# Retention's scores and values from rounded halves in three passes, q and k kept in the hidden tile, the gate's projection issued behind each head's values

## The reference

```python
def project(a, rope):
    q, k, v, g = jnp.split(a @ w_in, [hk, 2 * hk, 2 * hk + hv], axis=-1)
    ...
    if rope is not None:
        q, k = apply_rope(q, *rope), apply_rope(k, *rope)
    k = k * RET_DK ** -0.5
    ...
def readout(o, g):
    y = rms_norm_2(o).transpose(0, 2, 1, 3).reshape(B, n, hv).astype(g.dtype)
    return (jax.nn.silu(g) * y) @ w_out
```

## Time and profile before

| | |
|---|---|
| median of 3 runs | 3059.17 us (3057.82 to 3060.34) |
| the profiled execution | 3062.67 us, of which the span is 3060.9 us |
| TensorE busy | 2918.7 us, 95% of the span |
| VectorE, ScalarE, GpSimd busy | 1477.6, 1044.0, 535.0 us |
| DMA | 268.81 MB, mean 88 GB/s |

### The profile page before, as it was taken

How to read it: one execution, slowest core, us unless ns; L and a number is a source line. 1 busy time by engine, 2 the same in 40 slices (tenths; PEclk the granted TensorE clock), 3 DMA queues, 4 the chain that set the end, 5 groups by cost and what they waited for, 6 DMA issues and landing times.

```text
span 3060.9 us, 40191 instructions
## 1 busy us (share of the span) xinstructions
PE 2918.7 (95%) x16176; PEld 2480.4 (81%) x16176; DVE 1477.6 (48%) x2596; ACT 1044.0 (34%) x1813; POOL 535.0 (17%) x287
## 2 busy tenths in 40 slices
PE   7999989899998999999998899999998998999998
PEld 7888886888878868778685888888887777898887
DVE  5676569457674324242333735434564525642224
ACT  4322247442333422222222622122235535452222
POOL 1342200023231101111010011111102212012220
PEclk9999989899999999999999999999998999999999
DMA  3544312125443101111010023323312111122221
GB/s 137 177 158 169 107 64 74 65 90 173 149 160 123 58 28 62 49 48 63 28 62 21 29 90 119 102 74 109 128 49 89 56 57 66 63 76 105 102 95 37
DMA packets 84697, 268.81 MB, mean 88 GB/s; under 512 B 8992, under 2 KB 16544, under 8 KB 84128
## 3 DMA queue, kind: packets, MB, share of 16 engines
q1 hardware_dynamic: 84512, 266.25, 25.2%
HBM read 262.54 MB, written 2.10 MB: 86 GB/s over the span
## 4 chain that ended last, share of the span: by engine, by line
PE 61%; DVE 4%; ACT 2%; issue 1%; POOL 0%; DMA 0%; DVEq 0%; ACTq 0%; POOLq 0%; SPq 0%
PE ps L1348 18%; PE ps L1349 18%; PE ps L1350 18%; PE ps L1530 3%; PE ps L1580 1%; PE ps L1521 1%; PE ps L1564 1%; PE ps L1553 1%; ACT t_whi L1610 1%; DVE t_misc L1916 0%; ACT t_h L1659 0%; DVE t_x L1938 0%; DVE t_wlo L1896 0%; DVE t_tmp L2248 0%; DVE t_misc L2256 0%
## 5 line engine op out<-in xcount | busy, mean ns | idle before, releaser
L1348 PE MATMUL ps<-t_h,t_whi 128*128 128x512 f32 (+1 forms) x2368 | 830.2, 351 | 28.0 <-POOL t_wlo L2330 19.9
L1349 PE MATMUL ps<-t_h,t_wlo 128*128 128x512 f32 (+1 forms) x2368 | 825.5, 349 | 0.0
L1350 PE MATMUL ps<-t_h,t_whi 128*128 128x512 f32 (+1 forms) x2368 | 824.3, 348 | 0.0
L2330 POOL TENSOR_TENSOR t_wlo<-t_raw,t_whi 128x1024 fp32r<-128x1024 f32 (+3 forms) x147 | 356.6, 2426 | 1542.4 <-ACT t_whi L1610 1542.3
L1348 PEld LDWEIGHTS ps<-t_h,t_whi 128*128 128x128 f32 x2368 | 455.2, 192 | 90.5 <-issue 18.9
L1349 PEld LDWEIGHTS ps<-t_h,t_wlo 128*128 128x128 f32 x2368 | 455.5, 192 | 54.8
L1350 PEld LDWEIGHTS ps<-t_h,t_whi 128*128 128x128 f32 x2368 | 454.5, 192 | 55.4
L1348 PE MATMUL ps<-t_hid,t_whi 128*128 128x256 f32 (+1 forms) x1306 | 426.9, 327 | 11.2 <-DVE t_hid L2028 4.0
L1896 DVE TENSOR_TENSOR t_wlo<-t_raw,t_whi 128x1024 fp32r<-128x1024 f32 (+3 forms) x180 | 222.5, 1236 | 440.1 <-ACT t_whi L1610 439.9
L1610 ACT CAST t_whi<-t_raw 128x1024 fp32r<-128x1024 f32 (+3 forms) x327 | 326.3, 999 | 310.2 <-PE ps L1350 279.2
L1349 PE MATMUL ps<-t_hid,t_wlo 128*128 128x256 f32 (+1 forms) x1306 | 423.0, 324 | 0.0
(11 more groups left out here) (249 smaller groups left out, 3813.8 us busy)
## 6 DMA issues: line engine op xcount, KB each, us to landing
t_raw<-in_gu SPq DMA_DIRECT2D x176, 512.0 KB, 3.2
t_raw<-in_ada SPq DMA_DIRECT2D x96, 512.0 KB, 3.2
t_raw<-in_dn SPq DMA_DIRECT2D x52, 512.0 KB, 3.5
t_raw<-in_dn SPq DMA_DIRECT2D x24, 384.0 KB, 3.2
t_raw<-in_ret_v SPq DMA_DIRECT2D x16, 512.0 KB, 3.2
t_raw<-in_ret_qk SPq DMA_DIRECT2D x16, 512.0 KB, 3.2
t_raw<-in_ret_g SPq DMA_DIRECT2D x16, 512.0 KB, 3.1
t_raw<-in_ret_o SPq DMA_DIRECT2D x16, 512.0 KB, 3.5
```

What stands on the lines that cost most here:

```text
L1348: e.matmul(out, whi, xlo, start=first, stop=False, skip_group_check=shared)
L1349: e.matmul(out, wlo, xhi, start=False, stop=False, skip_group_check=shared)
L1350: return e.matmul(out, whi, xhi, start=False, stop=last, skip_group_check=shared)
L2330: e.tensor_tensor(m.block(1, it.slot, n), m.raw(it), m.block(0, it.slot, n), ALU.subtract).then_inc(*S["lo_pool"].of(j))
```

## The change

- The scores' and values' float32 matmuls become `products` of rounded halves. So q and k get a high half (ScalarE) and a low half (VectorE), written into `HID`, where the head's output y goes later; v gets both halves in the drain of its projection (`rows_split`); and the decayed scores p get a high half on ScalarE (`ret_score` there) and a low half on VectorE (`ret_low`).
- Scores and values of the context and the latents are put in one order written out by hand (`order`), with three places for p (`place`) and score banks 4, 5 and 7. A `ret_low` is put one score behind.
- q and k are projected in one batch of four weight blocks: the four latent groups first, then the four context groups. The scores follow at once.
- The gate's projection comes behind the values. One buffer per token segment holds the gate, and the second multiplication, the cast and the low half follow group by group (`ret_y`, `ret_split`). The latents' mean square is put behind its second group. For head 3 the segments are turned round, context first.
- `ret_setup` and the decays of head 0 come behind `v_rows(0)`.
- `M` gets an fp32r name for the same memory (`MW`).

```diff
-RQK, ROC, RVV, RPA, RST, RDI, RCS, RGG = 0, 3072, 4096, 7168, 8192, 9728, 10880, 11904
+RDI, RCS, RST, RSC, RVV, RVL, RPA, RSG, ROL, ROC = 0, 1152, 2176, 3712, 4096, 7168, 10240, 11264, 11904, 13952
...
-                put("rows_copy", g=g.id, bank=g.bank, after=after, key=(key, g.tt), dst=dest(g.tt))
+                put("rows_split" if low_dest else "rows_copy", g=g.id, bank=g.bank, after=after, key=(key, g.tt), dst=dest(g.tt),
...
     def retention():
+        n_head = 4
+        ov = {"qk": state["hid_free"], "v": state["misc_free"]}
+        order = [("s", 0, 0), ("s", 512, 0), ("s", 512, 1), ("s", 0, 1), ("v", 512, 0), ("v", 512, 1), ("s", 0, 2), ("v", 0, 0), ("s", 0, 3),
+                 ("v", 0, 1), ("s", 0, 4), ("v", 0, 2), ("s", 0, 5), ("v", 0, 3), ("v", 0, 4), ("v", 0, 5)]
+        place = {(0, 0): (0, 0), (512, 0): (1, 0), (512, 1): (1, 256), (0, 1): (2, 0), (0, 2): (1, 0), (0, 3): (0, 0), (0, 4): (2, 0), (0, 5): (1, 0)}
+        score_bank = {(0, 0): 4, (512, 0): 5, (512, 1): 7, (0, 1): 4, (0, 2): 5, (0, 3): 4, (0, 4): 5, (0, 5): 4}
...
+        def attend(h):
+
+            lows = []
+            for what, t0, i in order:
+                n, at, kt, last = (512, 256)[t0 == 512], place[t0, i], keys[t0][i], i == len(keys[t0]) - 1
+                if what == "s":
+                    b = score_bank[t0, i]
+                    if at[1] == 0:
+                        taken = ov["p"][at[0]]
+                        ov["p"][at[0]] = []
+                    put("ret_score", h=h, t0=t0, n=n, i=i, kt=kt, bank=b, at=at, before=seat(b, "drain_dve", ("ret_p", h, t0, i)), after=taken)
+                    lows.append(dict(h=h, t0=t0, n=n, i=i, at=at))
+                    while len(lows) > (1 if (t0, i) != (0, 5) else 0):
+                        put("ret_low", **lows.pop(0))
+                    continue
+                before = [owner.get(c, []) for c in range(4)] if i == 0 else [[]] * 4
+                put("ret_value", h=h, t0=t0, n=n, i=i, kt=kt, at=at, last=last, before=before)
+                if t0 == 0 or last:
+                    ov["p"][at[0]] = [("ret_ps", ("v", h, t0, i, 3))]
+                if last:
+                    for c in range(4):
+                        owner[c] = [("drain_act", ("ret_o", h, t0, c))]
+                    squares(h, t0, n, last_i=i)
+                if (t0, i) == (0, 1):
+                    finish(h, 512, 256)
+
+        t = {}
...
+        def gates(h):
+
+            seen = []
+
+            def value(i):
+                put("ret_y", **seen[i])
+
+            def split(i):
+                put("ret_split", over=[("ret_ps", ("s", h, 0, 5))] + ov["qk"], **seen[i])
+
+            def post(g, c):
+                i = len(seen)
+                seen.append(dict(h=h, c=c, t0=g.t0, n=g.n))
+                put("ret_g", g=g.id, bank=g.bank, after=ov["sg"][g.t0], **seen[i])
+                ov["sg"][g.t0] = [("ret_y", (h, c, g.t0))]
+                if i == 1:
+                    finish(h, 0, 512)
+                    value(0)
+                if i >= 1:
+                    value(i)
+                    split(i - 1)
+                if i == 7:
+                    split(i)
+
+            return columns([(("ret_g", h * 4 + c), (SLOT,), DC, ("h", 4), [(0, "drain_act", lambda g, c=c: post(g, c))]) for c in range(4)],
+                           SEG2[::-1] if h == n_head - 1 else SEG2)
+
+        v_rows(0)
         pro = state["misc_free"]
         put("ret_setup", after=pro)
...
-            if h == 0:
-                decays(0)
-
-            def g_post(g, c, h=h):
-                put("ret_g", c=c, h=h, g=g.id, bank=g.bank, t0=g.t0, n=g.n, after=ov["g"])
-
-            last_h = columns([(("ret_g", h * 4 + c), (SLOT,), DC, ("h", 4),
-                               [(0, "drain_act", lambda g, c=c: g_post(g, c))]) for c in range(4)], SEG2)
-            state["h_free"] = [last_h]
-
-            finish = None
-            for t0, n, tiles in ((512, 256, (4, 5)), (0, 512, (0, 1, 2, 3, 4, 5))):
-                def score(i, t0=t0, n=n, tiles=tiles):
...
-                for i in range(len(tiles) + 1):
-                    if i < len(tiles):
-                        score(i)
-                    if i >= 1:
-                        value(i - 1)
...
+            queries_keys(h)
+            attend(h)
             ov["v"] = [("ret_ps", ("v", h, 0, 5, 3))]
-            ov["st"] = [("ret_ps", ("s", h, 0, 5)), ("drain_dve", ("ret_p", h, 0, 5)), ("drain_dve", ("ret_p", h, 0, 4))]
-            if h < 3:
-                def once(fn):
-                    fn()
-                    yield from ()
-                chains[3] = [5.0, once(finish)]
+            ov["st"] = [("drain_dve", ("ret_p", h, 0, 5))]
+            state["h_free"] = [gates(h)]
+            ov["oc"] = [("ret_lo", (h, t0, 3)) for t0 in (512, 0)]
+            ov["p"][2] = ov["p"][2] + ov["oc"]
+            state["acc_free"] = ov["oc"]
+            if h < n_head - 1:
                 v_rows(h + 1)
                 decays(h + 1)
-            else:
-                finish()
-            ov["g"] = [("ret_lo", (h, t, 3)) for t in (512, 0)]
...
+    def ret_qk(self, part, w, k, t0, n):
+
+        return self.hid(part, w * 2 + k, 768, t0, n)
...
+    def ret_p(self, part, at, n):
+
+        i, o = at
+        if i < 2:
+            return self.HID[:, part * 4096 + 3072 + i * 512 + o:part * 4096 + 3072 + i * 512 + o + n]
+        return self.MW[:, ROL + part * 512 + o:ROL + part * 512 + o + n]
 
...
-            else:
-                w.wait_ge("drain_act", ("qkc", it.h, 1, k))
+            for ww, lat in ((0, it.t0 < 512), (1, it.kt < 4)):
+                if lat:
+                    w.wait_ge("qk_lo", (it.h, ww, k))
+                else:
+                    w.wait_ge("drain_dve", ("qkc", it.h, ww, k))
             if k == 0:
                 wait_all(it.before)
-            done = e.matmul(m.PS[:, it.bank, 0:it.n], m.qk(1, k, it.kt * P, P), m.qk(0, k, it.t0, it.n), start=k == 0, stop=k == 1)
...
-        pw = m.at(RPA + (it.i % 2) * 512, it.n)
-        w.wait_ge("drain_dve", ("ret_p", it.h, it.t0, it.i))
-        w.wait_ge("drain_act", (("ret_v", it.h), it.kt))
+        w.wait_ge("p_lo", (it.h, it.t0, it.i))
+        w.wait_ge("drain_dve", (("ret_v", it.h), it.kt))
         for c in range(4):
             wait_all(it.before[c])
-            done = e.matmul(m.PS[:, c, 0:it.n], m.at(RVV + it.kt * 512 + c * P, P), pw, start=it.i == 0, stop=it.last)
+            done = products(m.PS[:, c, 0:it.n], m.ret_v(0, it.kt, c), m.ret_v(1, it.kt, c), m.ret_p(0, it.at, it.n), m.ret_p(1, it.at, it.n),
+                            it.i == 0, it.last)
             if it.last or c == 3:
...
         wait_all(it.after)
-        e.copy(m.qk(it.w, it.k, 512, 256), m.PS[:, it.bank, 0:256]).then_inc(*S["drain_act"].of(it.g, ("qkc", it.h, it.w, it.k)))
+        e.copy(m.ret_qk(0, it.w, it.k, 512, 256), m.PS[:, it.bank, 0:256]).then_inc(*S["qk_hi"].of((it.h, it.w, it.k, "ctx")))
+
+    def qk_rope(it):
+        wait_all(it.after)
+        for half in range(2):
+            w.wait_ge("qk", (it.h, it.w, half))
+            e.copy(m.ret_qk(0, it.w, half, 0, 512), m.tmp(it.offs[half * 2], 512)).then_inc(*S["qk_hi"].of((it.h, it.w, half)))
+
+    def ret_score(it):
+        w.wait_ge("drain_dve", ("ret_p", it.h, it.t0, it.i))
+        wait_all(it.after)
+        e.copy(m.ret_p(0, it.at, it.n), m.ret_raw(it.at, it.n)).then_inc(*S["p_hi"].of((it.h, it.t0, it.i)))
...
+    def ret_split(it):
+        w.wait_ge("ret_y", (it.h, it.c, it.t0))
+        wait_all(it.over)
+        e.copy(m.hid(0, it.c, 768, it.t0, it.n), m.ret_o(it.c, it.t0, it.n)).then_inc(*S["ret_act"].of(("hi", it.h, it.t0, it.c)))
...
+            e.tensor_tensor(u, u, v, ALU.subtract if half == 0 else ALU.add).then_inc(*S["qk"].of((h, wq, half)))
+        wait_all(it.after)
+        for half in range(2):
+            w.wait_ge("qk_hi", (h, wq, half))
+            hi = m.ret_qk(0, wq, half, 0, 512)
+            e.tensor_tensor(m.ret_qk(1, wq, half, 0, 512), m.tmp(it.offs[half * 2], 512), hi, ALU.subtract).then_inc(*S["qk_lo"].of((h, wq, half)))
...
+    def rows_split(it):
+        w.wait_ge("drain_act", it.key)
+        wait_all(it.after)
+        e.tensor_tensor(m.MW[:, it.low:it.low + 512], m.PS[:, it.bank, :], m.MW[:, it.dst:it.dst + 512], ALU.subtract).then_inc(
+            *S["drain_dve"].of(it.g, it.key))
...
+    def ret_low(it):
+        w.wait_ge("p_hi", (it.h, it.t0, it.i))
+        e.tensor_tensor(m.ret_p(1, it.at, it.n), m.ret_raw(it.at, it.n), m.ret_p(0, it.at, it.n), ALU.subtract).then_inc(*S["p_lo"].of((it.h, it.t0, it.i)))
...
+    def ret_y(it):
+        h, t0, c = it.h, it.t0, it.c
+        o = m.ret_o(c, t0, it.n)
         w.wait_ge("ret_dve", ("rs", h, t0))
-        for c in range(5):
-            if c < 4:
-                o, g = m.ret_o(c, t0, n), m.at(RGG + c * 768 + t0, n)
-                e.tensor_tensor(o, o, rs, ALU.mult).then_inc(*S["ret_n"].of((h, t0, c)))
...
```

(5 more changed lines are left out.)

187 lines of the change are left out of this document (83 added, 104 removed).

## The result

| | before | changed |
|---|---|---|
| median, us | 3058.49 (3057.74 to 3060.34, 4 runs) | 3009.02 (3007.05 to 3010.04, 4 runs) |
| ratio | | 0.9837, 95% interval 0.9820 to 0.9854 |
| span of the profiled execution | 3060.9 | 3005.4 |

The changed kernel is faster by 49.5 us. The forecast was 3018.1, a gain of 41.1, with a range of 3006 to 3037: right in sign and kind, and 9 us too high. In the traces 5.0 of the 55.5 lie ahead of retention, in code that is the same: the v projection of head 0 starts at 983.94 in the one and at 978.92 in the other, and between 979 and 984 in all traces of this study, whatever the kernel (981.43 in the second trace of the changed kernel itself).

What follows compares the result with a forecast made beforehand. TensorE, busy 95% of the span, was taken as the bound. Terms -29.0 - 9.6 - 4.9 + 2.4 = -41.1 against the profiled 3062.7 gave 3021.6, less 3.5 for the median: 3018.1 us, range 3006 to 3037.

Steps and rivals of the forecast that it cites:

- The passes: Scores and values: three rounded passes replace each exact float32 product, all on TensorE's path; -29.0 us.
- Head 3's end: Bare reciprocal, multiplications, casts and low halves get cover beside the gate's projection; 1.1 us of wait left; -9.6 us.
- The chain of f2: Norm chain ahead of retention: two table loads and the Exp leave ScalarE, root sooner, half-clock stretch goes; -4.9 us.
- The new waits: Inside retention: 11.8 us of new TensorE waits less 9.4 of old ones; +2.4 us, between -8 and +11.
- the front: Norm chain at head 0's v projection, the term called the chain of f2; -4.9 us.
- The heads' starts: First decayed score and first value wait behind low halves: 2.25 us per head, four heads, 9.0; bounds 0 and 15.
- The gate's first group: Waits for a bank that ret_copy empties, 0.8 us in heads 0 and 3; 1.6 us.
- The v block: Next v block prepared late behind the gate's last drains, 0.4 x 3; 1.2 us, bounds 0 and 4.
- The rival's mechanism: Two gaps of about 1.1 us at each head's start bring half clock; +10, 3028 us; chance 0.15.
- The slower rival: Order gives p's round trip through three engines no cover: 32 x 2.7 = +86, 3104 us; chance 0.03.
- The rival in which the heads' starts cost nothing: ScalarE and VectorE run ahead at the heads' starts: 9.0 less, 3009 us; chance 0.13.
- The rival in which only the passes pay: Norm chain and head 3's end gain nothing: -29.0 + 2.4, 3032.5 us; chance 0.15, with cases keeping one gain.

Runs made afterwards that it cites:

- The float32 run: Changed kernel with scores and values as one exact float32 product each in place of three rounded passes, casts and low halves kept: 3038.35 us.
- the run with the setup moved alone: Kernel before with one edit, ret_setup put behind v_rows(0): 3054.52 us against 3058.33, ratio 0.9987.
- Both experiments on it: Changed kernel with the small Exp back ahead of v_rows(0): 3016.65 us; kernel before with only ret_setup moved behind v_rows(0): 3054.52 us.
- the run with the low half later: Changed kernel with the weight block's low half moved from ahead of the first decayed score to behind each head's fourth score: 3006.84 us.
- the run without the lag: Changed kernel with each ret_low directly behind its own score on VectorE, not behind the next one: 3014.11 us, ratio to before 0.9861.
- the two-pass run: Changed kernel without the pass of the low halves of k and v in scores and values: 2983.31 us.

## Why the prediction was right, and where it was off

**The passes (-29.0): right.** In head 1, scores and values take 38.50 us before, with 2.30 of waits in it, and 29.42 in the changed kernel without one: 6.8 us, 27.1 in four heads. The float32 run gives 26.5 + 2.7 = 29.2 for the exchange by the retention stretch, and 27.9 + 2.7 = 30.6 by the medians. The forecast lies between.

**Head 3's end (-9.6): right.** In the traces -10.0: the wait of 2.45 at L1537, 1.43 in the two matmuls of the mean square (half clock and 0.5 of wait), and 6.15 in the output projection up to the norm. What was to be left, 1.1 us, is there with that size and that cause (L2332), and the clock is 1.00 around it.

**The chain of f2 (-4.9): right, -5.4.** The wait vanished in place of falling to 0.7, and the stretch at half clock went. In the run with the setup moved alone the wait is 0.33, so the root came 2.7 us sooner, and not 2.35. In the changed kernel's trace more of the work behind the first wait runs at half clock (from the start of the sum's eight matmuls to the next matmul it takes 1.72 us, and 0.92 in that run), and this fills the rest: VectorE has written the row by 991.81, and TensorE comes to it at 992.07. Both experiments on it agree.

**The new waits (+2.4): this is the step that failed.** They are 5.2 us and not 11.8, so that the term is -4.2. Of the 7.4 us between the forecast sum and the -48.5 of the traces it makes 6.6. The passes gave 1.9 less than forecast, head 3's end and the front 0.4 and 0.5 more, and 1.8 us, 0.4 or so per head, are left over. The starts of the blocks say where they lie, in head 1: the v projection takes 32.7 us and not 33.5, the context's mean square 0.68 and not 0.87, and the projections of q, k and the gate together 0.5 more, without waits. The latents' mean square stood inside the v projection and stands inside the gate's now; that this is the cause was not tested. Three values in the term:

- *The heads' starts, 9.0, measured 3.7.* The cause was right in three heads, as the run with the low half later shows, and its size off. VectorE in head 0:

```profile
1054.62 1.23 DVE L1945 TENSOR_TENSOR t_wlo<-t_raw,t_whi 128x1024 fp32r<-128x1024 f32 x1 [0.59 <-ACT t_whi L1642]
1055.77 1.02 DVE L2303 SCALAR_TENSOR_TENSOR t_m<-ps,t_m 128x512 f32<-128x512 f32 x2
1057.14 0.69 DVE L2308 TENSOR_TENSOR t_hid<-t_m,t_hid 128x512 fp32r<-128x512 f32 x1 [0.35 <-ACT t_hid L1847]
```

```profile
1056.51 0.50 PE L1382 MATMUL ps<-t_hid 128*128 128x512 f32 x1 [0.53 <-DVE t_m L2303]
...
1058.55 0.38 PE L1382 MATMUL ps<-t_hid,t_mw 128*128 128x256 f32 x1 [0.37 <-DVE t_hid L2308]
```

  The scores begin at 1053.00, the first is done near 1054.4, and the weight's low half starts at 1054.62, so that the decayed score is late by its 1.2 us. I took 1.1 of that as exposed. But three scores of 2.8 us stand ahead of the fourth and end near 1055.9, only 0.5 ahead of the bank. And the second wait was counted as if the first had not already given 0.5 us of cover to the same chain: two waits on one chain were added at full price each. The second price does not come out of its own terms either: the cast's 0.62 and the subtraction's 0.4 to 0.69, less 1.36, are at or below nothing, and not 1.15. What the recorded sum left out is VectorE's queue: between the first decayed score and the low half that the first value needs it runs two more decayed scores and another low half, from 1055.77 to 1058.50. Head 1 has none of the two, since a wait of 1.0 for bank 4, which the last context group of k holds, stands ahead of its first score. That is a wait that I had not seen: I followed the banks of the gate's groups and not those of the scores.
- *The gate's first group, 1.6, measured 1.5*, in heads 0 and 3 as forecast.
- *The v block, 1.2, measured 0*: no wait stands at its weights.

**The rivals.** The clock did not fall at the heads' starts: it is 1.00 in all four heads, with waits of 0.53 and 0.37 in three of them, and it held with 0.53 and 0.95 in the run without the lag. The rival's mechanism is real, though. With 1.4 and 0.9 us, in the two-pass run, it fell in two heads of three. The Trainium skill ("TensorE: Matmul & The Clock Gate", section "A second HAM failure mode: psum-queue depth-cycling") would have it fall for micro-idles between groups. The heads go through the banks here and keep the full clock at waits of half a microsecond and, in one run, of 0.95, so in this kernel what the page describes shows at larger gaps alone, and not at all of these. The slower rival was priced at 3104 and forecast on an order that the change doesn't have; built, that order gave 3108, with less waiting (2.16 per tile and not 2.7) and some 28 us, mostly of clock, that the 86 did not hold: that the two numbers lie so close is luck. What kept the change from it is the written order, and 2 us of it the lag. The rival in which the heads' starts cost nothing was priced at 3009, which is the time measured, by luck too: the starts cost 3.7 us, and the rest came from the other terms. The rival in which only the passes pay fell with head 3's end and the front, 15.4 us between them.
